# The first head group's decay matrices, built from transferred gate sums on VectorE in place of masked products on TensorE

## The reference

```python
g = -jnp.exp(a_log) * jax.nn.softplus(a_in + dt_bias)      # one gate per token and head, 16 heads
gc = jnp.cumsum(g, axis=-1)                                # running sums inside a chunk of 64 tokens
diff = gc[..., :, None] - gc[..., None, :]
decay = jnp.exp(jnp.where(tri_incl, diff, -jnp.inf))       # 64x64 for each head and chunk
lower = jnp.where(tri_strict, einsum(k_beta, k) * decay, 0.0)
sol = triangular_solve(eye + lower, [v_beta, k_beta * exp(gc)])
qk = einsum(q, k) * decay
```

## Time and profile before

| what | value |
|---|---|
| median of 3 runs | 2354.98 us (2354.83 to 2355.15) |
| profiled execution, its own time | 2354.94 us |
| its span (first to last instruction) | 2353.2 us |
| busy: PE, DVE, ACT, POOL | 2342.6, 1517.1, 1223.3, 63.7 us |
| weights and all else moved | 432.66 MB, mean 184 GB/s |
| granted TensorE clock | 1.0 |

### The profile page before, as it was taken

How to read it: one execution, slowest core, us unless ns; L and a number is a source line. 1 busy time by engine, 2 the same in 40 slices (tenths; PEclk the granted TensorE clock), 3 DMA queues, 4 the chain that set the end, 5 groups by cost and what they waited for, 6 DMA issues and landing times.

```text
span 2353.2 us, 35087 instructions
## 1 busy us (share of the span) xinstructions
PE 2342.6 (100%) x12183; PEld 1963.4 (83%) x12183; DVE 1517.1 (64%) x2146; ACT 1223.3 (52%) x1931; POOL 63.7 (3%) x92
## 2 busy tenths in 40 slices
PE   9999999999999999999999999999999999999999
PEld 7887788888888888888888878888887888888887
DVE  5657655556577775477776668787876755555554
ACT  5445544444465554355554475756465455555543
POOL 0011100000100000000000000000000000000000
PEclk9999999999999999999999999999999999999999
DMA  8766565565756655666655655555554585656555
GB/s 272 218 207 179 170 191 191 180 198 186 223 179 196 191 185 197 184 196 188 193 186 189 192 154 169 153 169 151 161 149 147 181 225 163 192 156 187 169 169 172
DMA packets 289497, 432.66 MB, mean 184 GB/s; under 512 B 32976, under 2 KB 129136, under 8 KB 289264
## 3 DMA queue, kind: packets, MB, share of 16 engines
q1 hardware_dynamic: 282976, 422.69, 58.5%
q10 hardware_dynamic: 6416, 8.56, 1.2%
HBM read 429.07 MB, written 7.10 MB: 185 GB/s over the span
## 4 chain that ended last, share of the span: by engine, by line
PE 95%; DVE 2%; ACT 1%; DVEq 1%; issue 0%; DMA 0%; ACTq 0%
PE gemm L557 22%; PE gemm L559 22%; PE gemm L558 22%; PE gemm L542 7%; PE aux L542 7%; PE gemm L535 3%; PE aux L535 3%; PE aux L1937 2%; DVE w_lo L502 1%; PE aux L559 1%; PE aux L558 1%; PE aux L557 1%; ACT w_hi L492 0%; PE aux L2178 0%; PE aux L2397 0%; PE aux L2378 0%
## 5 line engine op out<-in xcount | busy, mean ns | idle before, releaser
L502 DVE TENSOR_TENSOR w_lo<-raw,w_hi 128x1024 fp32r<-128x1024 f32 (+1 forms) x800 | 959.3, 1208 | 570.4 <-ACT w_hi L492 565.3
L492 ACT ACTIVATE w_hi<-raw 128x1024 fp32r<-128x1024 f32 (+1 forms) x800 | 815.8, 1042 | 506.6 <-PE gemm L559 402.1
L557 PE MATMUL gemm<-w_lo,hT 128*128 128x512 f32 x1600 | 637.0, 398 | 0.1
L559 PE MATMUL gemm<-w_hi,hT 128*128 128x512 f32 x1600 | 624.1, 390 | 0.0
L558 PE MATMUL gemm<-w_hi,hT 128*128 128x512 f32 x1600 | 623.3, 390 | 0.0
L557 PEld LDWEIGHTS gemm<-w_lo,hT 128*128 128x128 f32 x1600 | 300.6, 188 | 63.7 <-issue 4.1
L559 PEld LDWEIGHTS gemm<-w_hi,hT 128*128 128x128 f32 x1600 | 300.3, 188 | 63.8
L558 PEld LDWEIGHTS gemm<-w_hi,hT 128*128 128x128 f32 x1600 | 300.9, 188 | 58.8 <-issue 0.2
L542 PE MATMUL gemm<-hT,w_hi 128*128 128x512 f32 x704 | 218.2, 393 | 0.0
L542 PE MATMUL aux<-hT,w_hi 128*128 128x512 f32 x672 | 208.0, 390 | 0.0
L557 PE MATMUL gemm<-w_lo,yT_hi 128*128 128x512 f32 x472 | 184.2, 390 | 0.5 <-DVE yT_lo L1465 0.5
(11 more groups left out here) (341 smaller groups left out, 2277.3 us busy)
## 6 DMA issues: line engine op xcount, KB each, us to landing
raw<-in_w_up SPq DMA_DIRECT2D x336, 256.0 KB, 3.0
raw<-in_w_in SPq DMA_DIRECT2D x144, 512.0 KB, 4.3
raw<-in_a_w_in SPq DMA_DIRECT2D x128, 512.0 KB, 3.7
raw<-in_b_w_in SPq DMA_DIRECT2D x128, 512.0 KB, 4.3
raw<-in_w_down SPq DMA_DIRECT2D x76, 512.0 KB, 4.7
raw<-in_w_branch SPq DMA_DIRECT2D x32, 512.0 KB, 4.6
raw<-in_w_out SPq DMA_DIRECT2D x32, 512.0 KB, 4.8
raw<-in_a_w_out SPq DMA_DIRECT2D x32, 512.0 KB, 3.8
```

The source lines that it names most:

```text
L492: nc.scalar.activation(hi, src, ACT.Copy).then_inc(S("hi_done"), 1)
L502: nc.vector.tensor_tensor(lo, src, hi.bitcast(F32), ALU.subtract).then_inc(S("lo_done"), 1)
L557: nc.tensor.matmul(dst, xh, wl[:, k, :], start=h["start"] and k == 0, stop=False)
L559: mm = nc.tensor.matmul(dst, xl, wh[:, k, :], start=False, stop=h["stop"] and k == h["n"] - 1)
```

## The change

Three things replace the first group's own way. ACT, behind the write of `gc_rows`, waits for it and issues the spread of the first four heads' rows into `gc_all`; two steps later it waits for `d_arg` and takes the exponent of `dec` in one instruction. DVE has the 8 subtractions of the later groups (now a function, `decay_arguments`) as a last step of its `decays()`, two steps behind the sums' copies. The masked product on DVE, the two products on PE and the exponent from the banks are gone. The counts of `d_arg` and `gc_spread` in `delta` move by one.

```diff
@@ ACT, delta(gi)
-                    act.wait_ge(S("d_arg"), gi + 1)
+                    act.wait_ge(S("d_arg"), gi + 2)
@@ ACT, decays()
                 act.dma_start(gc_rows.rearrange("t h c -> (t h) c"), gcT[:, :]).then_inc(S("gc_written"), 16)
                 yield
-                act.wait_ge(S("d_arg0"), 1)
-                for tb in range(TB):
-                    A(dec[:, tb * HG:(tb + 1) * HG, :], AX[2 + tb][:, :].rearrange("p (a c) -> p a c", c=P), ACT.Exp)
+                act.wait_ge(S("gc_written"), 16)
+                act.dma_start(gc_all[:, :, :].rearrange("p (t h) c -> p t (h c)", t=TB),
+                              gc_rows[:, 0:HG, :].rearrange("t h c -> t (h c)").partition_broadcast(P)).then_inc(S("gc_spread"), 16)
+                yield
+                yield
+                act.wait_ge(S("d_arg"), 1)
+                A(dec[:, :, :], dec[:, :, :], ACT.Exp)
                 yield
@@ DVE
+            def decay_arguments(first):
+
+                for tb in range(TB):
+                    for h in range(HG):
+                        e = V.tensor_scalar(dec[:, tb * HG + h, :], gc_all[:, tb * HG + h, :],
+                                            gcs[:, tb, bass.ds(first + h, 1)], 0.0, ALU.subtract, ALU.min)
+                e.then_inc(S("d_arg"), 1)
@@ DVE, delta(gi)
-                    dve.wait_ge(S("gc_spread"), gi * 16 + 16)
-                    for tb in range(TB):
-                        for h in range(HG):
-                            e = V.tensor_scalar(dec[:, tb * HG + h, :], gc_all[:, tb * HG + h, :],
-                                                gcs[:, tb, bass.ds(gi * HG + (HG + h), 1)], 0.0, ALU.subtract, ALU.min)
-                    e.then_inc(S("d_arg"), 1)
+                    dve.wait_ge(S("gc_spread"), gi * 16 + 32)
+                    decay_arguments(gi * HG + HG)
@@ DVE, decays()
                 e.then_inc(S("ab_g"), 1)
                 yield
-                dve.drain()
-                dve.wait_ge(S("chunk_masks"), 1)
-                for tb in range(TB):
-                    e = V.tensor_tensor(dec[:, tb * HG:(tb + 1) * HG, :], rep(m_le[:, :], HG), each(gg[:, tb, 0:HG], P), ALU.mult)
-                e.then_inc(S("d_gm"), 1)
                 yield
                 yield
                 dve.wait_ge(S("gc_done"), 1)
@@
                 V.tensor_tensor(edec[:, :, :], gx[:, :, :], AX[3][:, P:P + TB * H].rearrange("p (t h) -> p t h", t=TB),
                                 ALU.subtract).then_inc(S("g_rest"), 1)
+                yield
+                yield
+                dve.wait_ge(S("gc_spread"), 16)
+                decay_arguments(0)
                 yield
@@ PE, decays()
-                pe.wait_ge(S("gc_kept"), 1)
-                pe.wait_ge(S("d_gm"), 1)
-                for tb in range(TB):
-                    m = MM(AX[2 + tb][:, :], m_gt[:, :], dec[:, tb * HG:(tb + 1) * HG, :].rearrange("p a c -> p (a c)"),
-                           start=True, stop=True)
-                m.then_inc(S("d_arg0"), 1)
-                yield
```

## The result

| | before | changed |
|---|---|---|
| median | 2355.06 us (2354.66 to 2355.81, 20 runs) | 2357.91 us (2357.01 to 2359.93, 20 runs) |
| profiled execution, its span | 2354.94, 2353.2 us | 2357.87, 2356.1 us |

The ratio is 1.0013, with a 95% interval from 1.0007 to 1.0019: 2.9 us slower, within the 0.2% that the prediction called unseen, though with so many runs the sign is clear. The changed kernel's runs also spread over 2.9 us, those of before over 1.2 us.

A forecast was written before the change was run, and what follows sets the result against it. PE bounds the kernel, busy for 2342.6 of 2353.2 us. Removing 2.8 us from PE and adding a 4.1 us stall gives +1.3 us on 2354.94 us: 2356.3 us, +0.06%, range 2354.7 to 2358.8 us.

The forecast's parts named there:

- the likeliest case: PE stalls before the tile's last half with no change of clock: +1.3 us, 2355.5 to 2357.5 us, chance 0.66.
- the first rival: The stall cools TensorE, so matmuls behind it run at half clock, 1.8 us more: +3.1 us, 2358.1 us, chance 0.15.
- The saving on PE: At L2336 on PE, about 1.0 us of wait and 1.8 us of products go: 2.79 us.
- The chain through memory: Write of the turned sums takes 3.5 us, then the spread 5.8 us, landing at 1413.26 while DVE waits.
- The stall: PE waits 4.1 us for the sixth `w_lo`, starting the tile's last half at 1416.2, not 1412.12.
- What comes behind: At the tile's end DVE leaves 2.7 us late and PE 1.3 us late; nothing added, up to 0.5 us for range.
- the cover: DVE's thinnest lead over PE up to 1446, 1.5 us, just covers DVE coming 1.4 us nearer to PE.
- fast transfers: The spread takes no more than a weight load, 3.7 us; PE ends 0.8 us ahead, 2354.2 us; chance 0.11.
- entirely hidden, with -2.8 us: The spread lands by 1409.2, less than 2 us after issue, so PE keeps the full saving; chance 0.03.
- The rule on chained transfers: Counting about 2 us fixed per transfer, write and spread take 4 us instead of 9.3; the change gains 2.8 us.

The follow-up runs named there:

- kernel with the clock kept up: The changed kernel with four extra 512-column products on PE, never read, in the gap before the tile's last half: 2356.24 us, ratio 1.0005.
- kernel with the later wait: The changed kernel with DVE's wait and eight subtractions two steps later, between the seventh and eighth `w_lo`: 2357.04 us, ratio 1.0008.

## Why the prediction was right, and where it was not

The measured 2357.91 us lies in the range of 2354.7 to 2358.8 us, and within 0.2% of before, as forecast with 0.93. But the likeliest case was +1.3 us at full clock, and what happened is the first rival, +3.1 us, to which I gave 0.15. The range, which reaches over both, caught the number; the forecast's own mechanism had the clock wrong.

- **The saving on PE**: 2.79 us forecast. The transposes behind moved from 1408.57 to 1405.88, which with the 0.14 us of this execution is 2.8 us. Right.
- **The chain through memory**: write 3.5 us forecast, 2.8 us found; spread 5.8 us forecast, 6.3 us found. By luck the two errors nearly cancel, and DVE begins the subtractions at 1413.18, for a forecast of 1413.26.
- **The stall**: the last half at 1416.2 forecast, 1416.03 found. Right, and with it the reading that the sixth `w_lo` is the half that PE needs next. The kernel with the clock kept up, which has the stall alone, is at +1.0 us for the forecast's +1.3.
- **The clock**: the failed step is the choice between the forecast and its rival, "The forecast, a stall with no change of clock [...]: 0.66". The fall cost 1.6 us in the trace and 1.8 us by the kernel that kept TensorE busy; the rival's price from the earlier trace rows, 1.8 us, was right. I had the only measured waits, up to 1.8 us, as the bound of what leaves the clock alone, and no reason to put a stall twice as long at 0.15. By TensorE: Matmul & The Clock Gate (Part 1) of the Trainium skill, idle gaps of about this length are to be avoided; the trace agrees, at 3.65, 3.31 and 5.05 us of idle time, and I had leaned on the lack of a row instead.
- **What comes behind**: DVE 2.7 us late as it leaves the tile, forecast; 2.60 us by its next instruction, 1418.16 for the 1415.56 of before. No second wait, forecast, and none appeared; in the changed kernel the cover was not tried, as the slow clock made PE later still. In the kernel that kept TensorE busy it was: DVE leaves the tile 2.8 us later than before (1418.34 for 1415.56, 0.3 us of it shift), PE is 1.5 us later, and up to 1460 us PE waits for no `w_lo` behind the one of 0.28 us at 1416.21.
- **Rival "fast transfers", "entirely hidden, with -2.8 us"**: this price was wrong. The kernel with the products gone and no transfer at all gains 2.0 us, since PE then catches up with DVE in the loop's first tile. I had found that lead of 1.5 us, and used it only as a cover for lateness of DVE; it is just as much a cap on what PE can gain. In the order of the changed kernel, where ACT's exponent stands two halves later, the cap is lower still: with no wait for the transfer on DVE at all the gain is 0.3 us, so the 0.8 us that this rival gives for a spread of 3.7 us was too much as well.
- **The rule on chained transfers**: The section of the Trainium skill that it rests on (DMA: Bandwidth & Descriptors, "Anatomy of one DMA") describes transfers issued by GpSimd, and those here are issued by ACT. Measured are 2.8 us for the write and 6.3 us for the spread, and the full 2.8 us would not have come even with both as short as that estimate has them: without any wait for them it is the 0.3 us above.

## What to carry to other kernels

Where an engine works ahead for another, its lead is the budget for every wait put into its stream, and also the most that the other engine can win: look for the thinnest lead behind the change before counting a saving in full. A chain of two transfers took 9.1 us in the changed kernel and from 7.7 to 10.2 us in the others, so when its first transfer is issued decides most: issued 3 us sooner, the same idea was 3.9 us faster than the changed kernel and by its median 1.1 us faster than the kernel before. Where the result was used moved the time too, by 1.0 us for the better (two steps later) and 1.6 us for the worse (one step earlier). And the three stalls of 3.3 to 5.1 us on an otherwise busy TensorE cost their length plus 1.5 to 1.6 us for the matmuls at the lower clock behind them.

## What the runs showed of the hardware

- The clock fell behind idle gaps of 3.65, 3.31 and 5.05 us, and stayed at 1.00 behind those of 0.5, 1.1 and 0.3 us. Each fall was followed by 3.0 to 3.4 us of matmuls 0.43 us apart. In the kernel with the later wait two matmuls behind the gap were still 0.23 us apart (1425.90 to 1426.13) before the clock fell.
- The spread of 512 KB took between 4.9 and 7.3 us over all kernels, the write of 16 KB between 2.8 and 4.0 us: 4.0 us in both kernels that issued it 3 us sooner, 3.5 us in the kernel before, 2.8 or 2.9 us in the others. The first spread took least, 4.9 us, where no weight load was issued while it ran, and most, 7.3 us, with three.
- PE-side work that is never read, 3.6 us of it, made the changed kernel 1.8 us faster.
